# Two attentions in one kernel: the products with v move in front of the turns, and each group's last steps move a unit or two later

## The chip, the cores and the metric

The kernel is one program on one NeuronCore of a Trainium2 chip. TensorE, VectorE, ScalarE, GpSimd and the DMA queues run their own instruction lists, written out by hand, and meet only at semaphores. The metric is the device time of one execution in microseconds; smaller is better. The kernel before takes 2598.61 us (median of 3 runs, 2598.22 to 2599.84).

## The reference

The reference is a stack of three transformer-like layers over 512 latent tokens and 256 context tokens of width 1024. The change touches only its two softmax attentions:

```python
def one_block(qi):                       # 128 queries of one head
    s = einsum('bqhgd,bkhd->bhgqk', qi, k) * scale
    p = softmax(s, axis=-1)
    return einsum('bhgqk,bkhe->bqhge', p, v)
```

- The first layer (GQA) has 16 heads of 64. The 512 latent tokens attend to all 768 keys, the 256 context tokens to the 256 context keys.
- The second layer (MLA) has 16 heads. The 512 latent tokens attend to 768 keys.

Projections, MLPs, layer norms and the third layer (gated linear attention, mLSTM and an S5 state space) make up the rest of the time and are not changed.

## The kernel before, in words

A **unit** is one head and one block of 128 queries. MLA has 64 units, all with 768 keys. GQA has 96: 64 latent ones with 768 keys and 32 context ones with 256, in the order latent, latent, context. Four units of one kind that share a block of queries form a **group**. Operands are kept as two bf16 halves (high and low), so most products are three matmuls (lines 326, 327, 328).

Each unit passes through these steps:

| step in the code | engine | work for a unit with 768 keys | line |
|---|---|---|---|
| `scores` S | TensorE | 128x768 scores into a pair of PSUM banks | 1062, 1063 (GQA), 326 to 328 (MLA) |
| `largest` | VectorE | the negated row maximum | 1167 |
| `exponent` | ScalarE | exp of the scores, into one of three buffers | 1117, 1121 |
| `turn` T | TensorE | six 128x128 transposes, in two parts of three, one PSUM bank each | 1074 |
| `high` | ScalarE | the high half of each part, from PSUM | 1128 |
| `low` | VectorE | the low half of each part, which frees that part's bank | 1173 |
| `weigh` W | TensorE | 18 small products with v, into the group's bank | 326 to 328 |

After the fourth unit of a group come `divide` (VectorE, lines 1154 or 1156 and 1161), `out_turn` (TensorE, two transposes, line 1092), `out_high` (ScalarE, 1132) and `out_low` (VectorE, 1178), which frees the bank of `out_turn`.

The **bank rings** set what may run ahead. `bank(e, ring, name)` takes the next bank of a ring in turn and makes TensorE wait until its last user is freed. The ring "T" has two banks, 4 and 5, and serves the parts of `turn` and the `out_turn` of a group alike. The ring "S" has two pairs (0, 1) and (2, 3). "O" is bank 6 and "O2" bank 7. A latent unit's turn takes both T banks, a context unit's one, an `out_turn` one.

Each engine has its own loop over steps `i`, and the order inside a step is the order of its queue. With u for the last unit of a group, the kernel before has:

- TensorE (lines 1095 to 1103): S(i), T(i-2), W(i-3), then `out_turn` where i-6 = u.
- ScalarE (1134 to 1143): `exponent`(i-1), `high`(i-2), a quarter of a weight tile in four steps (i = 6, 10, 14, 18), `out_high` where i-6 = u.
- VectorE (1180 to 1190): `divide` where i-4 = u, `largest`(i), `low`(i-2), a quarter in the same four steps, `out_low` where i-6 = u.

Of the kernel before, what the change touches and what calls it, by code (L numbers as in the profile page):

```python
# [131 lines left out]
def build(nc, a, out):  # L132
    ctx = ExitStack()
    with ctx:
# [851 lines left out]
        class Pass:  # L986


            def __init__(self, tag, qtiles, keys, OT, q, k, v, O, sums, stacked):
                self.tag, self.qtiles, self.keys, self.OT = tag, qtiles, keys, OT  # L990
                self.q, self.k, self.v, self.O, self.sums0 = q, k, v, O, sums

                self.stacked, self.width = stacked, 65 if stacked else 64
                self.nq, self.nk = len(qtiles), keys[1] // 128
                self.parts = [(0, 3), (3, 6)] if self.nk == 6 else [(0, self.nk)]
# [20 lines left out]
        class Attention:  # L1016


            def __init__(self, tag, order, P, PT):
                self.tag, self.order, self.P, self.PT = tag, order, P, PT  # L1020
                self.n = len(order)
                self.steps = self.n + 7

            def scores_at(self, u):
                return at(("S", self.tag, u), self.order[u][0].keys[1])
# [24 lines left out]
        def attention_pe(e, Q):  # L1050
            t = Q.tag

            def scores(u):
                A, r = Q.order[u]
                h, j = A.unit(r)
                q, k = A.q(e, h, A.qtiles[j]), A.k(e, h)
                bank(e, "S", ("S", t, u))
                k0, n = A.keys
                for c0, c1 in [(0, 512), (512, n)] if n > 512 else [(0, n)]:
                    o, x = at(("S", t, u), c1 - c0, c0), [x[:, k0 + c0:k0 + c1] for x in k]  # L1060
                    if A.stacked:
                        e.matmul(o, q, x[0], start=True, stop=False)
                        m = e.matmul(o, q, x[1], start=False, stop=True)
                    else:
                        m = mm3(e, o, q, x, True, True)
                m.then_inc(pe.sem, pe.mark(("S", t, u)))

            def turn(u):
                A, _ = Q.order[u]
                ac.wait_ge(e, ("exp", t, u))  # L1070
                for i, (a_, b_) in enumerate(A.parts):
                    bank(e, "T", ("T", t, u, i))
                    for k in range(a_, b_):
                        m = e.transpose(at(("T", t, u, i), 128, (k - a_) * 128), Q.p(u)[:, k * 128:(k + 1) * 128], ident)  # L1074
                    m.then_inc(pe.sem, pe.mark(("T", t, u, i)))

            def weigh(u):
                A, r = Q.order[u]
                h, j = A.unit(r)
                if r % 4 == 0:  # L1080
                    bank(e, A.O, ("O", A.tag, r // 4))
                o = at(("O", A.tag, r // 4), A.width, A.width * (r % 4))
                dv.wait_ge(e, ("low", t, u))
                for k in range(A.nk):
                    m = mm3(e, o, [Q.PT[u % 3][:, i, k, :] for i in range(2)], A.v(e, k, h), k == 0, k == A.nk - 1)
                m.then_inc(pe.sem, pe.mark(("W", t, u), *([("O", A.tag, r // 4)] if r % 4 == 3 else [])))

            def out_turn(A, g):
                bank(e, "T", ("OT", A.tag, g))
                dv.wait_ge(e, ("out", A.tag, g))  # L1090
                for k in range(2):
                    m = e.transpose(at(("OT", A.tag, g), 128, k * 128), A.OT[g % 2][:, k * 128:(k + 1) * 128], ident)
                m.then_inc(pe.sem, pe.mark(("OT", A.tag, g)))

            for i in range(Q.steps):
                if i < Q.n:
                    scores(i)
                if 0 <= i - 2 < Q.n:
                    turn(i - 2)
                if 0 <= i - 3 < Q.n:  # L1100
                    weigh(i - 3)
                if whole := Q.group_at(i - 6):
                    out_turn(*whole)


# [2 lines left out]
        def attention_act(e, Q, done):  # L1108
            t = Q.tag

            def exponent(u):
                A, r = Q.order[u]
                if u > 2:
                    pe.wait_ge(e, ("T", t, u - 3, Q.last_part(u - 3)))
                dv.wait_ge(e, ("max", t, u))
                if A.stacked:
                    e.activation(Q.p(u), Q.scores_at(u), EXP, bias=Q.largest(u)).then_inc(ac.sem, ac.mark(("exp", t, u), ("free", ("S", t, u))))  # L1117
                    return
                if r > 7:
                    dv.wait_ge(e, ("out", A.tag, r // 4 - 2))  # L1120
                e.activation(Q.p(u), Q.scores_at(u), EXP, bias=Q.largest(u), accum_out=A.sums(r)).then_inc(ac.sem, ac.mark(("exp", t, u), ("free", ("S", t, u))))  # L1121

            def high(u):
                for i in range(len(Q.order[u][0].parts)):
                    if u > 2:
                        pe.wait_ge(e, ("W", t, u - 3))
                    pe.wait_ge(e, ("T", t, u, i))
                    e.activation(Q.pt(u, i)[0], Q.turned_at(u, i), COPY).then_inc(ac.sem, ac.mark(("high", t, u, i)))  # L1128

            def out_high(A, g):  # L1130
                pe.wait_ge(e, ("OT", A.tag, g))
                e.activation(A.out(g)[0], at(("OT", A.tag, g), 256).rearrange("p (k n) -> p k n", n=128), COPY).then_inc(ac.sem, ac.mark(("out high", A.tag, g)))

            for i in range(Q.steps):
                if 0 <= i - 1 < Q.n:
                    exponent(i - 1)
                if 0 <= i - 2 < Q.n:
                    high(i - 2)
                if i in QUARTERS:
                    pe.wait_ge(e, done)  # L1140
                    high_quarter(e, QUARTERS[i])
                if whole := Q.group_at(i - 6):
                    out_high(*whole)

        def attention_dve(e, Q):
            t = Q.tag

            def divide(u, A, g):

                sums = A.sums(4 * g, 4)  # L1150
                ac.wait_ge(e, ("exp", t, u))
                if A.stacked:
                    pe.wait_ge(e, ("O", A.tag, g))
                    e.reciprocal(sums, A.O_at(g)[:, :, 64]).then_inc(dv.sem, dv.mark())
                else:
                    e.reciprocal(sums, sums).then_inc(dv.sem, dv.mark())
                    pe.wait_ge(e, ("O", A.tag, g))
                if g > 1:
                    pe.wait_ge(e, ("OT", A.tag, g - 2))
                dv.wait_ge(e)  # L1160
                e.tensor_tensor(A.OT[g % 2].rearrange("p (h n) -> p h n", n=64), A.O_at(g)[:, :, 0:64], sums.unsqueeze(2).to_broadcast([128, 4, 64]), MUL).then_inc(dv.sem, dv.mark(("out", A.tag, g), ("free", ("O", A.tag, g))))

            def largest(u):
                if u > 3:
                    ac.wait_ge(e, ("exp", t, u - 4))
                pe.wait_ge(e, ("S", t, u))
                e.tensor_reduce(Q.largest(u), Q.scores_at(u), AX.X, MAX, negate=True).then_inc(dv.sem, dv.mark(("max", t, u)))  # L1167

            def low(u):
                for i in range(len(Q.order[u][0].parts)):  # L1170
                    hi, lo = Q.pt(u, i)
                    ac.wait_ge(e, ("high", t, u, i))
                    e.tensor_tensor(lo, Q.turned_at(u, i), hi, SUB).then_inc(dv.sem, dv.mark(("low", t, u), ("free", ("T", t, u, i))))  # L1173

            def out_low(A, g):
                hi, lo = A.out(g)
                ac.wait_ge(e, ("out high", A.tag, g))
                e.tensor_tensor(lo, at(("OT", A.tag, g), 256).rearrange("p (k n) -> p k n", n=128), hi, SUB).then_inc(dv.sem, dv.mark(("o", A.tag, g), ("free", ("OT", A.tag, g))))

            for i in range(Q.steps):  # L1180
                if whole := Q.group_at(i - 4):
                    divide(i - 4, *whole)
                if i < Q.n:
                    largest(i)
                if 0 <= i - 2 < Q.n:
                    low(i - 2)
                if i in QUARTERS:
                    low_quarter(e, QUARTERS[i])
                if whole := Q.group_at(i - 6):
                    out_low(*whole)  # L1190


# [930 lines left out]
        def mla_pe(e):  # L2123
            heads_pe(e)
            attention_pe(e, MLA)
# [1610 lines left out]
```

## Time and profile before

| | before |
|---|---|
| median of 3 runs | 2598.61 us |
| the profiled execution | 2602.68 us |
| its span | 2600.9 us |
| TensorE matmul busy | 2470.7 us (95%) |
| VectorE busy | 1630.2 us (63%) |
| ScalarE busy | 1039.5 us (40%) |
| mean granted TensorE clock | 0.985 of full speed |

The time of an execution is its span plus 1.8 us outside it. The two attentions fill the span from 179 to 362 us (GQA) and from 1109 to 1262 us (MLA). In the trace, PE is the matmul and PEld the weight load ahead of it. The time in brackets behind a row is the idle time just before it and what ended that.

### The profile page before, as it was taken

What the parts mean: (1) busy time and instruction counts of PE and PEld (TensorE: products, weight loads), DVE (VectorE), ACT (ScalarE), POOL (GpSimd) and SP (SyncE); (2) the same over time, 40 slices, a digit from 0 to 9 for tenths busy, and PEclk for the clock granted to TensorE, in tenths of its full rate; (3) what the DMA queues carried; (4) which work ended last, traced back from release to release, by engine and by line L of the source; (5) the groups of instructions that cost most, each with busy time, mean ns of one, the idle gap of its engine ahead of it and who ended that gap; (6) DMA issues with size and microseconds to landing.
All of it is one profiled execution on the core that took longest, in us unless ns stands there. A gap on an engine that the chain in (4) does not pass through costs nothing.

```text
span 2600.9 us, 39022 instructions
## 1 busy us (share of the span) xinstructions
PE 2470.7 (95%) x16410; PEld 1439.0 (55%) x16410; DVE 1630.2 (63%) x2478; ACT 1039.5 (40%) x1666; POOL 727.5 (28%) x789
## 2 busy tenths in 40 slices
PE   6999999999999999899989999999999999999999
PEld 3566665665565585477554444735644445744444
DVE  4469964868844345888677744479966774533341
ACT  3457753433311124677444322333352234523230
POOL 0210000649999603300041000016454552011100
PEclk8999999999999999999999999999999999999999
DMA  6520014124444331300236645232212323233340
GB/s 246 180 80 18 2 50 146 52 88 146 154 154 162 138 122 47 106 18 2 61 102 201 203 163 178 79 106 69 86 57 92 111 100 118 66 95 99 99 146 33
DMA packets 224046, 271.40 MB, mean 104 GB/s; under 512 B 10047, under 2 KB 181438, under 8 KB 220798
## 3 DMA queue, kind: packets, MB, share of 16 engines
q1 hardware_dynamic: 217486, 247.05, 29.5%
q0 software_dynamic: 5280, 18.64, 2.0%
q8 instruction: 129, 2.11, 0.3%
q10 hardware_dynamic: 1104, 3.21, 0.3%
q14 instruction: 47, 0.39, 0.0%
HBM read 252.62 MB, written 10.49 MB: 101 GB/s over the span
## 4 chain that ended last, share of the span: by engine, by line
PE 74%; DVE 15%; ACT 6%; issue 2%; DMA 2%; POOL 1%; ACTq 0%; DVEq 0%; POOLq 0%
PE PS L326 22%; PE PS L328 21%; PE PS L327 21%; PE PS L1074 2%; DVE WB L305 2%; DVE SM L1167 2%; ACT WB L293 2%; DVE AR L1173 2%; ACT AR L1117 1%; DMA WS<-in_w_ada 1%; DVE X L1450 1%; PE PS L558 1%; DVE GT L1459 1%; DMA WS<-in_mlp_w 1%; DMA EB<-in_s_lam_im 1%
## 5 line engine op out<-in xcount | busy, mean ns | idle before, releaser
L326 PE MATMUL PS<-H,WB 128*128 128x512 bf16 (+1 forms) x1976 | 686.4, 347 | 20.8 <-DVE WB L305 8.0
L327 PE MATMUL PS<-H,WB 128*128 128x512 bf16 (+1 forms) x1976 | 685.5, 347 | 0.0
L328 PE MATMUL PS<-H,WB 128*128 128x512 bf16 (+1 forms) x1976 | 684.9, 347 | 0.0
L305 DVE TENSOR_TENSOR WB<-WS,WB 128x2048 bf16<-128x2048 f32 (+2 forms) x154 | 348.2, 2262 | 265.6 <-ACT WB L293 265.5
L293 ACT ACTIVATE WB<-WS 128x2048 bf16<-128x2048 f32 (+2 forms) x154 | 275.1, 1787 | 399.5 <-PE PS L328 222.9
L326 PE MATMUL PS<-AR,WB 128*128 128x512 bf16 (+1 forms) x1140 | 369.9, 324 | 8.9 <-DVE WB L305 8.1
L327 PE MATMUL PS<-AR,WB 128*128 128x512 bf16 (+1 forms) x1140 | 369.6, 324 | 0.0
L328 PE MATMUL PS<-AR,WB 128*128 128x512 bf16 (+1 forms) x1140 | 369.6, 324 | 0.0
L326 PEld LDWEIGHTS PS<-H,WB 128*128 128x128 bf16 x1976 | 194.9, 99 | 214.3 <-issue 22.0
L328 PEld LDWEIGHTS PS<-H,WB 128*128 128x128 bf16 x1976 | 194.9, 99 | 167.1 <-issue 3.0
L327 PEld LDWEIGHTS PS<-H,WB 128*128 128x128 bf16 x1976 | 195.0, 99 | 163.3 <-issue 5.3
L1538 POOL TENSOR_TENSOR X<-X,STAT 128x256 f32<-128x256 f32 x56 | 57.5, 1062 | 660.7 <-DVE H L1467 660.7
L326 PEld LDWEIGHTS PS<-AR,WB 128*128 128x128 bf16 x1140 | 111.6, 98 | 97.0 <-issue 13.0
L658 DVE SCALAR_TENSOR_TENSOR ACC<-WS,SIL,ACC 128x512 f32<-128x512 f32 x196 | 152.6, 797 | 14.5 <-DMA WS<-in_w_ada 8.9
L327 PEld LDWEIGHTS PS<-AR,WB 128*128 128x128 bf16 x1140 | 111.7, 98 | 72.1 <-issue 2.5
L328 PEld LDWEIGHTS PS<-AR,WB 128*128 128x128 bf16 x1140 | 111.6, 98 | 71.8 <-issue 0.6
L1173 DVE TENSOR_TENSOR AR<-PS,AR 128x384 bf16<-128x384 f32 x288 | 143.3, 534 | 12.1 <-ACT AR L1128 10.0
L1167 DVE TENSOR_REDUCE SM<-PS 128x1 f32<-128x768 f32 x160 | 135.2, 846 | 10.7 <-PE PS L328 6.1
L1128 ACT ACTIVATE AR<-PS 128x384 bf16<-128x384 f32 x288 | 127.2, 477 | 34.3 <-PE PS L1074 29.9
L1438 DVE SCALAR_TENSOR_TENSOR X<-PS,MOD,X 128x256 f32<-128x256 f32 (+1 forms) x56 | 33.4, 596 | 170.7 <-PE PS L328 170.6
L1599 ACT ACTIVATE GT<-PS 128x512 f32<-128x512 f32 x96 | 50.2, 523 | 194.3 <-PE PS L328 185.1
L326 PE MATMUL PS<-AR 128*128 128x65 bf16 (+1 forms) x616 | 108.0, 233 | 1.9 <-ACT GT L1121 0.9
(497 smaller groups left out, 4293.1 us busy)
## 6 DMA issues: line engine op xcount, KB each, us to landing
WS<-in_mlp_w SPq DMA_DIRECT2D x64, 1024.0 KB, 5.7
WS<-in_w_ada SPq DMA_DIRECT2D x40, 1024.0 KB, 5.1
WS<-in_w_in SPq DMA_DIRECT2D x26, 1024.0 KB, 5.1
WS<-in_ada_w SPq DMA_DIRECT2D x24, 1024.0 KB, 5.2
WS<-in_ffn_w_in SPq DMA_DIRECT2D x44, 512.0 KB, 4.9
WS<-in_ffn_w_out SPq DMA_DIRECT2D x10, 1024.0 KB, 4.9
AR<-in_w_ada SPq DMA_DIRECT2D x8, 1024.0 KB, 13.0
e_scratch<-EB POOLq DMA_DIRECT2D x16, 512.0 KB, 3.1
```

The lines of the kernel that those rows point to most:

```text
L293: e.activation(hi, staged_as(i, hi), COPY).then_inc(ac.sem, ac.mark(("hi", i)))
L305: e.tensor_tensor(lo, staged_as(i, lo), hi, SUB).then_inc(dv.sem, dv.mark(("lo", i)))
L326: e.matmul(out_, l[0], r[0], start=start, stop=False)
L327: e.matmul(out_, l[0], r[1], start=False, stop=False)
L328: return e.matmul(out_, l[1], r[0], start=False, stop=stop)
L658: e.scalar_tensor_tensor(out=y, in0=w[:, x, :], scalar=s, in1=y, op0=MUL, op1=ADD).then_inc(dv.sem, dv.mark(("weighed", r, t // 2, v, k), ...
L1074: m = e.transpose(at(("T", t, u, i), 128, (k - a_) * 128), Q.p(u)[:, k * 128:(k + 1) * 128], ident)
L1128: e.activation(Q.pt(u, i)[0], Q.turned_at(u, i), COPY).then_inc(ac.sem, ac.mark(("high", t, u, i)))
L1167: e.tensor_reduce(Q.largest(u), Q.scores_at(u), AX.X, MAX, negate=True).then_inc(dv.sem, dv.mark(("max", t, u)))
L1173: e.tensor_tensor(lo, Q.turned_at(u, i), hi, SUB).then_inc(dv.sem, dv.mark(("low", t, u), ("free", ("T", t, u, i))))
L1538: e.tensor_tensor(seg(X, f, p), seg(X, f, p), factor_at(p), MUL).then_inc(po.sem, po.mark(("over", tag, f, p), ("factor read", tag)))
L1599: e.activation(x, ps(bank_of[("w1", i), m, s], SEG[s][1]), RELU).then_inc(ac.sem, ac.mark(("relu", i, n), ("free", (("w1", i), m, s))))
```

## The change

`Attention.steps` grows by two, and the order inside a step changes on the three engines:

```diff
-                self.steps = self.n + 7
+                self.steps = self.n + 9
@@ attention_pe
                 if i < Q.n:
                     scores(i)
+                if 0 <= i - 4 < Q.n:
+                    weigh(i - 4)
                 if 0 <= i - 2 < Q.n:
                     turn(i - 2)
-                if 0 <= i - 3 < Q.n:
-                    weigh(i - 3)
-                if whole := Q.group_at(i - 6):
+                if whole := Q.group_at(i - 7):
                     out_turn(*whole)
@@ attention_act
-                if 0 <= i - 1 < Q.n:
-                    exponent(i - 1)
-                if 0 <= i - 2 < Q.n:
-                    high(i - 2)
+                if 0 <= i - 3 < Q.n:
+                    high(i - 3)
                 if i in QUARTERS:
                     pe.wait_ge(e, done)
                     high_quarter(e, QUARTERS[i])
-                if whole := Q.group_at(i - 6):
+                if whole := Q.group_at(i - 8):
                     out_high(*whole)
+                if 0 <= i - 1 < Q.n:
+                    exponent(i - 1)
@@ attention_dve
-                if whole := Q.group_at(i - 4):
-                    divide(i - 4, *whole)
+                if whole := Q.group_at(i - 5):
+                    divide(i - 5, *whole)
+                if 0 <= i - 3 < Q.n:
+                    low(i - 3)
                 if i < Q.n:
                     largest(i)
-                if 0 <= i - 2 < Q.n:
-                    low(i - 2)
                 if i in QUARTERS:
                     low_quarter(e, QUARTERS[i])
-                if whole := Q.group_at(i - 6):
+                if whole := Q.group_at(i - 8):
                     out_low(*whole)
```

No instruction, DMA, buffer or bank is added or removed. The waits inside each step's function stay as they were.

## Rows read from the trace of the kernel before

**Rows 1.** Stretches: start to end, length, busy time of each engine, clock, DMA.
```profile
260.00:280.00 20.00, 18.56 (x240) 13.38 (x238) 18.21 (x38) 15.72 (x31) 0.00 (x0) 1.00 0.01 2
1076.70:1085.50 8.80, 6.47 (x33) 3.04 (x31) 7.75 (x14) 4.05 (x8) 8.49 (x7) 1.00 0.31 74
1085.60:1092.40 6.80, 5.26 (x13) 1.94 (x14) 4.74 (x6) 2.60 (x5) 6.80 (x12) 0.50 0.90 294
1200.00:1220.00 20.00, 19.33 (x269) 15.69 (x268) 17.98 (x33) 16.08 (x37) 0.00 (x0) 1.00 0.01 2
```

**Rows 2.** Waits of the GQA attention: total us, times, longest.
```profile
PEld PS L1074 <- DVE AR L1173: 26.4, 85, 1.0
```

**Rows 3.** Timeline of the MLA attention around an out_turn: start, length, engine, operation.
```profile
1202.90 0.38 PE L326 MATMUL PS<-AR 128*128 128x512 bf16 x1
...
1203.77 0.69 PEld L1074 LDWEIGHTS PS<-KM,GT 128*128 128x128 f32 x6
...
1204.40 0.87 ACT L1128 ACTIVATE AR<-PS 128x384 bf16<-128x384 f32 x2 [0.40 <-PE PS L1074]
...
1204.53 0.19 PE L326 MATMUL PS<-X,AR 128*128 128x64 bf16 x1
...
1204.95 1.01 DVE L1173 TENSOR_TENSOR AR<-PS,AR 128x384 bf16<-128x384 f32 x2
...
1205.03 0.19 PE L328 MATMUL PS<-EB,AR 128*128 128x64 bf16 x1
...
1205.56 0.20 PEld L1092 LDWEIGHTS PS<-KM,AR 128*128 128x128 f32 x2 [0.46 <-DVE AR L1173]
...
1205.83 0.38 PE L326 MATMUL PS<-AR 128*128 128x512 bf16 x1
...
1207.01 0.96 DVE L1167 TENSOR_REDUCE SM<-PS 128x1 f32<-128x768 f32 x1
...
1207.88 1.01 DVE L1173 TENSOR_TENSOR AR<-PS,AR 128x384 bf16<-128x384 f32 x2
```

**Rows 4.** Chain of waits in the GQA attention: the same turn, 12 units apart.
```profile
240.59 1.01 PE PS L1074 x6
...
263.33 1.01 PE PS L1074 x6
```

**Rows 5.** Timeline of the GQA attention: spacing and hand-over of each kind of operation.
```profile
267.01 0.42 DVE L1178 TENSOR_TENSOR H<-PS,H 128x256 bf16<-128x256 f32 x1
...
267.35 0.41 DVE L1167 TENSOR_REDUCE SM<-PS 128x1 f32<-128x256 f32 x1
267.49 0.31 PEld L1074 LDWEIGHTS PS<-KM,AR 128*128 128x128 f32 x3 [0.26 <-DVE H L1178]
267.66 0.91 ACT L1128 ACTIVATE AR<-PS 128x384 bf16<-128x384 f32 x2
...
268.18 1.02 DVE L1173 TENSOR_TENSOR AR<-PS,AR 128x384 bf16<-128x384 f32 x2 [0.41 <-ACT AR L1128]
...
268.79 0.31 PEld L1074 LDWEIGHTS PS<-KM,AR 128*128 128x128 f32 x3 [0.20 <-DVE AR L1173]
...
269.12 0.95 DVE L1167 TENSOR_REDUCE SM<-PS 128x1 f32<-128x768 f32 x1
...
269.38 0.95 ACT L1128 ACTIVATE AR<-PS 128x384 bf16<-128x384 f32 x2 [0.45 <-PE PS L1074]
...
271.05 0.96 DVE L1167 TENSOR_REDUCE SM<-PS 128x1 f32<-128x768 f32 x1
...
272.04 0.90 ACT L1117 ACTIVATE AR<-PS,SM 128x768 f32<-128x768 f32 x1 [0.39 <-DVE SM L1167]
...
272.26 0.17 DVE L1154 RECIPROCAL SM<-PS 128x4 f32<-128x4 f32 x1
...
272.81 0.41 DVE L1167 TENSOR_REDUCE SM<-PS 128x1 f32<-128x256 f32 x1
272.84 0.86 ACT L1128 ACTIVATE AR<-PS 128x384 bf16<-128x384 f32 x2
```

**Rows 6.** Lines in both attentions: count, busy us, mean ns, idle before.
```profile
L321 DVE TENSOR_TENSOR WB<-WS,WB 128x512 bf16<-128x512 f32 x8 | 5.5, 682 | 0.0
```

## The prediction, made before the change was run

> **What bounds the kernel now.** I read the table of stretches first, to see which engine limits each attention [rows 1]. Then came the waits and the timelines of one steady period of each. In the MLA attention TensorE is the bound. A unit takes S 0.97, T 0.65 and W 0.53 us, matmul start to matmul start: 1202.90 to 1204.53 is S and T together, 1204.53 to 1205.06 the 18 products [rows 3]. These follow each other without a gap, 2.155 us a unit. The only gap stands ahead of `out_turn`: its weight load waits 0.50 us (1205.06 to 1205.56) for a T bank, which VectorE's `low` must free. With 0.27 us for `out_turn` a group of four takes 4 x 2.155 + 0.27 + 0.50 = 9.39 us.
>
> In the GQA attention no engine is full. Twelve units (8 latent, 4 context, 3 groups) take 22.74 us [rows 4]. TensorE waits 26.4 us in all on `low` ahead of a turn [rows 2]. VectorE's own spacings are 0.94 us for a latent `low` (268.18 to 269.12), 0.87 for its maximum (the next one [rows 3] shows), about 0.34 for each context operation and for `out_low`, 0.55 for `divide` (272.26 to 272.81) [rows 5]. That gives 8 x 1.81 + 4 x 0.68 + 3 x 0.55 + 3 x 0.34 = 19.9 of 22.74 us. The rest is hand-overs between the engines.
>
> **What the edits really move.** A step's boundary is nothing to an engine; only the order of its queue counts. So I write out each queue across the steps.
>
> - ScalarE before: `exponent`(i-1), `high`(i-2), `exponent`(i), `high`(i-1). After: `high`(i-3), `exponent`(i-1), `high`(i-2), `exponent`(i). It is the same sequence, cut at another place. I cost this edit at nothing.
> - VectorE likewise: `largest` and `low` alternate with the same offset before and after. Nothing again.
> - TensorE before: T(i-2), W(i-3), S(i+1), T(i-1). After: T(i-2), S(i+1), W(i-3), T(i-1). S and W trade places; from one turn to the next there is still one S and one W. Scores are ready 0.53 us earlier, and W has 0.97 us more slack. W waits for nothing that its turn did not already wait for (both need `low`), and in MLA no S or W waits now, so the trade gives nothing there. In GQA it can take away VectorE's wait for scores. The timeline has it small, and the walk below counts it.
> - `divide` moves one instruction later, behind `largest`(u+4). The next group's first W still comes S and T (1.62 us) after W(u). `divide` starts 0.87 us later than before and ends in time. Nothing.
> - `out_turn` before stood behind T(u+4) and W(u+3). Now it stands directly behind T(u+5). This is the first cost.
> - `out_low` before stood right behind `low`(u+4). Now it stands behind `low`(u+5) and then `largest`(u+8), whose scores TensorE issues only after that `out_turn`. This is the second cost.
>
> **MLA, step by step.** Let 0 be the weight load of T(u+5). A turn's load to `high` is 0.63 us, `high` to `low` 0.55, `low` to the load that its bank frees 0.61, together 1.79 [rows 3]. `out_turn` takes the bank of the first part of the turn just issued, so it starts at 1.79 in both kernels. Before, TensorE had T and W to issue meanwhile and was ready at 1.29; now only T, and is ready at 0.76. The wait grows from 0.50 to 1.03: **0.53 us more a group**.
>
> The scores S(u+8) then start at 1.79 + 0.27 = 2.06. `largest`(u+8) starts 1.18 later (1205.83 to 1207.01) at 3.24, and VectorE is idle until then. `out_low` follows 0.87 later, at 4.11. The bank is free for a load 0.48 after its start (267.01 to 267.49 [rows 5]), at 4.59. The second part of T(u+6) needs that bank. Without a wait its load would go at 2.06 + 0.97 + 0.53 - 0.11 + 0.33 = 3.78, and by matmul starts (3.89 against 4.59, plus some 0.05 that a stalled load isn't overlapped) the loss is **0.75 us a group**. Before, this didn't arise, since `out_low` was done 0.9 us after `out_turn` began.
>
> What follows catches up with nothing, since TensorE is the bound: T(u+7), T(u+8) and T(u+9) come 2.155 us apart with their inputs ready. A period becomes 9.39 + 0.53 + 0.75 = 10.67 us. 14 groups have scores behind their `out_turn`; the last two fall into the drain. 14 x 1.28 = 17.9 us. Four steps convert a quarter of a weight tile (0.68 us on VectorE [rows 6]). These now stand ahead of `low`, beside the wait for scores. From their place I take 0.3 us less for each, -1.2 us, with 0 and -2.7 (all four hidden) as bounds. MLA: **+16.7 us**.
>
> **GQA, step by step.** Here stalls overlap with other waits, so I walked a period of 12 units by the spacings of [rows 3, 5]. The hand-overs: turn's load to `high` 0.59, `high` to `low` 0.52, `low` to load 0.61, `out_low` to load 0.48, maximum to `exponent` 0.99, `exponent` to the next `high` 0.80. For scores to maximum I take 0.86: MLA's 1.18 less a third of 0.97, as GQA scores are four matmuls and not six. `out_turn` costs 0.19 here. Before, the `out_turn` of the groups that end on the 5th and 11th unit of a period stood behind a context unit's turn, which takes one bank only, so that the other was long free; only the third waited. Now all three stand right behind a latent turn. The path that ends last, from `high` of one latent unit to the same 12 units on:
>
> - through the first `out_turn`, scores, maximum, `out_low`, second part of the next turn: 0.52 + 0.61 + 0.19 + 0.86 + 0.87 + 0.48 + 0.59 + 0.52 = 4.64;
> - VectorE and ScalarE in turn up to the next latent `low`: 0.47 + 0.99 + 0.80 + 0.52 = 2.78;
> - 0.94 + 0.87 + 0.55 (`divide`) + 0.94 + 0.99 + 0.80 + 0.52 = 5.61;
> - through the second `out_turn`, as the first: 4.12;
> - through the third, whose wait runs beside the second's: 0.47 + 0.87 + 3 x 0.34 + 0.55 = 2.91;
> - 0.94 + 0.87 + 0.94 + 0.99 + 0.80 = 4.54.
>
> The sum is 24.6 us against 22.74: **+1.86 us a period**. There are 8 periods, and the last is half drain: 7.5 x 1.86 = **+14.0 us**. Its bounds: 0 if the slack in this attention takes up both waits (26.4 us of waiting stand there), +20 if each of the 22 groups with scores behind costs 0.9, between the one wait and both of MLA.
>
> **Sum.** The profiled execution of 2602.68 us would become 2602.7 + 16.7 + 14.0 = 2633.4. It lies 4.1 us above the median of the runs, so the median becomes 2598.6 + 30.7 = **2629.3 us**. What follows each attention starts later by as much; the edits leave all DMAs alone, and the DMA share in both is 0.01 [rows 1], so no transfer is late.
>
> **A rule against the trace.** In MLA matmuls are busy 19.33 of 20 us and weight loads 15.69 [rows 1], and the unit's matmuls start without a gap [rows 3]. The Trainium skill (Perfetto Trace Analysis, Identifying the Most-Contended Engine) says that matmul busy time tells little of how near TensorE is to its limit, and that the busy share of weight loads, beside the FLOPs used, does. By that share, 78%, TensorE would have a fifth of its time to spare and an added wait of 1.28 us a group would be free, which is the second rival below. The spacing of the starts speaks against it.
>
> **Rivals.**
>
> - *One wait only* (+11 us, 2610). If `out_low` is not late, because scores come sooner than I count, MLA loses 14 x 0.53 = 7.4 and GQA about half of its slack-covered part, 4 us. For it: the second wait is a difference of two sums of six terms. Against: it is 0.7 us, far over their error. Chance 0.17.
> - *Waits hidden* (+0, 2598.6). The idle time of an engine with spare time takes them. Only GQA offers that. Chance 0.04.
> - *Faster* (2575 to 2590). The swap of S and W ends the GQA waits: at VectorE's 19.9 us a period, 8 x 2.84 = 23 us go, and it decides if VectorE's waits there came from late scores and not from the banks. It gives up to 2576 if MLA stays, 2592 if MLA loses 16.7. Against: TensorE's 26.4 us of waits are on `low`, that is on banks. Chance 0.07.
> - *The clock falls* (2650). In both attentions it is 1.00, at 18.56 busy us of 20 in GQA. It fell to 0.50 for 6.8 us behind a stretch with 2.3 idle us in 8.8 [rows 1]; my longest new gap is 1.0 us. If six of the 14 MLA groups ran such a stretch at half clock, each losing half of 6.8 us, 20 us come on top: 2650. The Trainium skill (TensorE: Matmul & The Clock Gate, A second HAM failure mode: psum-queue depth-cycling) says that short idles between groups of matmuls, from cycling PSUM banks, can make the clock swing between its levels; the trace shows such idles in GQA with no fall. Chance 0.06.
>
> **Chances.** The forecast has 0.66. The range for 8 in 10 reaches to the one-wait case and 11 us up: 2609 to 2640. A measurement here can't tell less than 0.2% (5.2 us) from no change. Faster 0.07, same 0.04, slower 0.89.
>
> **What would show it.** After: `out_turn`'s load waits about 1.0 us instead of 0.46 on `low` in MLA; a turn's second load waits 0.7 us on `out_low`, 14 times or more; the MLA period is 10.7 us and the GQA period 24.6; maxima of MLA wait for scores about 1.1 us once a group; clock 1.00 in both. Busy times stay. An `out_turn` that waits no longer than now, or a GQA period under 22.7, would prove me wrong.

## The result and the profile after

The changed kernel takes 2633.24 us (median of 4 runs, 2632.5 to 2634.67), the kernel before 2599.23 us beside it. The ratio is 1.0123 (95% interval 1.0111 to 1.0135): 1.2% slower. The forecast was 2629.3 us, 30.7 us on top of the median of the kernel before. The median grew by 34.0 us and the profiled execution by 30.8, from 2602.68 to 2633.45. That the second number meets the forecast to 0.1 us is partly luck: runs of the kernel before, taken for the experiments, lie between 2597.8 and 2605.8 us. The lengths of the two attentions, below, are the better test.

Where the time went, by stretch: I take the length of an attention from the start of its first maximum to the end of its last `out_low`.

| | GQA | MLA |
|---|---|---|
| before | 186.3 us | 156.3 us |
| after | 200.5 us | 173.4 us |
| difference, forecast | +14.2, +14.0 | +17.1, +16.7 |

Together +31.3 us; what lies outside both changed by -0.6 us between the two profiled executions. The same two stretches as in [rows 1], from the table of stretches of the changed kernel (start:end, length, busy us of PE, PEld, DVE, ACT, POOL, clock, DMA share, GB/s):

```profile
260.00:280.00 20.00, 16.06 (x208) 12.20 (x206) 15.83 (x33) 13.78 (x29) 0.00 (x0) 1.00 0.01 2
1200.00:1220.00 20.00, 17.32 (x223) 13.55 (x221) 15.75 (x28) 13.53 (x32) 0.00 (x0) 1.00 0.01 2
```

All engines are less busy in both, and the clock stays at 1.00, its upper level of 2.4 GHz. So the added time is idle time and not slower work.

**MLA after.** The timeline around one `out_turn` of the changed kernel, weight loads first, then VectorE. It answers to [rows 3].

```profile
1210.61 0.64 PEld L1074 LDWEIGHTS PS<-KM,STAT 128*128 128x128 f32 x6
1212.34 0.20 PEld L1092 LDWEIGHTS PS<-KM,AR 128*128 128x128 f32 x2 [1.08 <-DVE AR L1173]
1214.08 0.32 PEld L1074 LDWEIGHTS PS<-KM,GT 128*128 128x128 f32 x3
1215.13 0.31 PEld L1074 LDWEIGHTS PS<-KM,GT 128*128 128x128 f32 x3 [0.73 <-DVE H L1178]
1216.99 0.64 PEld L1074 LDWEIGHTS PS<-KM,GT 128*128 128x128 f32 x6
1219.18 0.64 PEld L1074 LDWEIGHTS PS<-KM,STAT 128*128 128x128 f32 x6
1221.37 0.64 PEld L1074 LDWEIGHTS PS<-KM,GT 128*128 128x128 f32 x6
```

```profile
1211.72 1.02 DVE L1173 TENSOR_TENSOR AR<-PS,AR 128x384 bf16<-128x384 f32 x2 [0.30 <-ACT AR L1128]
1213.79 0.96 DVE L1167 TENSOR_REDUCE SM<-PS 128x1 f32<-128x768 f32 x1 [1.04 <-PE PS L328]
1214.66 0.42 DVE L1178 TENSOR_TENSOR H<-PS,H 128x256 bf16<-128x256 f32 x1
...
1225.41 0.42 DVE L1178 TENSOR_TENSOR H<-PS,H 128x256 bf16<-128x256 f32 x1
```

Both new waits are there, one behind the other. The turn at 1210.61 is loaded in one piece. `out_turn` right behind it waits 1.08 us for `low` (0.46 before). Scores follow it, so VectorE has nothing to do for 1.04 us until 1213.79, does the maximum, and only then `out_low`. The next turn's second half, at 1215.13, waits 0.73 us for that `out_low`. From one `out_low` to the next is 10.75 us (1214.66 to 1225.41), where the prediction had 10.67. Over the whole attention the second wait stands there 14 times.

**GQA after.** The waits of the whole stretch (engine and line, what it waited for, us in total, times, longest), against 26.4 us of waits on `low` ahead of a turn in [rows 2]:

```profile
PEld PS L1092 <- DVE AR L1173: 19.8, 22, 1.3
PEld PS L1074 <- DVE H L1178: 16.2, 15, 1.7
...
PEld PS L1074 <- DVE AR L1173: 7.9, 34, 0.5
```

The waits of the turns on `low` fell by 18.5 us, those of `out_turn` on `low` and of the turns on `out_low` took their place. VectorE in this stretch, the same two operations 12 units apart:

```profile
265.48 0.96 DVE L1167 TENSOR_REDUCE SM<-PS 128x1 f32<-128x768 f32 x1 [0.72 <-PE PS L1063]
266.36 0.41 DVE L1178 TENSOR_TENSOR H<-PS,H 128x256 bf16<-128x256 f32 x1
...
290.18 0.96 DVE L1167 TENSOR_REDUCE SM<-PS 128x1 f32<-128x768 f32 x1 [0.72 <-PE PS L1063]
291.06 0.42 DVE L1178 TENSOR_TENSOR H<-PS,H 128x256 bf16<-128x256 f32 x1
```

The period is 24.70 us (265.48 to 290.18), forecast 24.6. Periods of 24.70 and 24.78 us alternate.

The six legs of the prediction's walk can be read off the same period. These rows are where they begin and end, from one `high` to the same one 12 units on:

```profile
263.23 0.86 ACT L1128 ACTIVATE AR<-PS 128x384 bf16<-128x384 f32 x2
267.93 0.56 DVE L1173 TENSOR_TENSOR AR<-PS,AR 128x384 bf16<-128x384 f32 x1 [0.70 <-ACT AR L1128]
270.88 1.02 DVE L1173 TENSOR_TENSOR AR<-PS,AR 128x384 bf16<-128x384 f32 x2
275.91 1.02 DVE L1173 TENSOR_TENSOR AR<-PS,AR 128x384 bf16<-128x384 f32 x2 [0.69 <-ACT AR L1128]
280.10 0.56 DVE L1173 TENSOR_TENSOR AR<-PS,AR 128x384 bf16<-128x384 f32 x1 [0.70 <-ACT AR L1128]
282.87 1.02 DVE L1173 TENSOR_TENSOR AR<-PS,AR 128x384 bf16<-128x384 f32 x2
287.93 0.86 ACT L1128 ACTIVATE AR<-PS 128x384 bf16<-128x384 f32 x2
```

They last 4.70, 2.95, 5.03, 4.19, 2.77 and 5.06 us; the prediction had 4.64, 2.78, 5.61, 4.12, 2.91 and 4.54. The path is the forecast one, but one `divide` (0.55 us) lies in the last leg and not in the third.

### The profile page after: what moved, and what is told of

Its sections match the earlier page's. It is cut to its first block, busy times and chain, and to the rows that moved or that the text cites. A ratio compares the mean times of both kernels' runs of the same rounds, so it can differ in the third digit from the quotient of the medians.

```text
span 2631.6 us, 39022 instructions
## 1 busy us (share of the span) xinstructions
PE 2471.7 (94%) x16410; PEld 1441.8 (55%) x16410; DVE 1631.4 (62%) x2478; ACT 1040.7 (40%) x1666; POOL 725.2 (28%) x789
## 4 chain that ended last, share of the span: by engine, by line
PE 71%; DVE 17%; ACT 6%; issue 2%; DMA 2%; POOL 1%; ACTq 0%; DVEq 0%; POOLq 0%
PE PS L326 21%; PE PS L328 21%; PE PS L327 21%; DVE SM L1167 3%; DVE AR L1173 2%; DVE WB L305 2%; PE PS L1074 2%; ACT WB L293 2%; ACT AR L1128 1%; ACT AR L1117 1%; DMA WS<-in_w_ada 1%; DMA WS<-in_mlp_w 1%; DVE X L1450 1%; PE PS L558 1%; DVE GT L1459 1%
```

## The experiments

Eight kernels were run. Each ratio is against runs of the kernel before on the same chip. The columns GQA and MLA are the lengths of the attentions in us in the profiled execution, taken as above; they separate effects that the total, with the runs of one kernel 2 to 10 us apart, can't. "Before" stands for the three sets of runs beside e1 to e4, e5 to e7 and e8; the changed kernel's ratio is against the 2599.23 us above. The MLA period is the steady one, without quarters.

| | median | ratio (95% interval) | GQA | MLA | MLA period |
|---|---|---|---|---|---|
| before | 2601.19 to 2601.72 in three sets | | 186.3 | 156.3 | 9.39 |
| after | 2633.24 | 1.0123 (1.0111 to 1.0135) | 200.5 | 173.4 | 10.75 |
| e1 | 2614.58 | 1.0050 (1.0035 to 1.0065) | 192.9 | 163.6 | 10.04 |
| e2 | 2603.54 | 1.0012 (1.0002 to 1.0021) | 180.9 | 165.2 | 10.04 |
| e3 | 2611.1 | 1.0038 (1.0023 to 1.0053) | 200.5 | 149.5 | 9.04 |
| e4 | 2591.52 | 0.9965 (0.9952 to 0.9977) | 186.3 | 148.7 | 8.87 |
| e5 | 2589.7 | 0.9956 (0.9944 to 0.9968) | 180.9 | 150.0 | 8.97 |
| e6 | 2582.46 | 0.9935 (0.9923 to 0.9947) | 174.8 | 150.0 | 8.97 |
| e7 | 2583.22 | 0.9933 (0.9921 to 0.9945) | 174.8 | 149.9 | 8.97 |
| e8 | 2582.6 | 0.9923 (0.9910 to 0.9937) | 174.9 | 148.7 | 8.87 |

### e1: the changed kernel, out_low in front of the maximum

```diff
                 if 0 <= i - 3 < Q.n:
                     low(i - 3)
+                if whole := Q.group_at(i - 8):
+                    out_low(*whole)
                 if i < Q.n:
                     largest(i)
...
-                if whole := Q.group_at(i - 8):
-                    out_low(*whole)
```

> The changed kernel with one edit: VectorE does out_low in front of largest in its step, and not behind it, so that it no longer waits for the scores behind out_turn. Theory (two waits, 0.5 and 0.75 us a group): the second wait goes, the first stays. MLA period 10.75 -> about 10.0 us (-10.5 us over 14 groups), a turn's second load no longer waits on out_low, the wait of out_turn's load stays at 1.1 us; GQA period 24.7 -> about 22.9 (-13 us). Total about 2610 us (2604 to 2618). Rival (one wait only: out_turn behind the turn is the whole cost, out_low's place costs nothing): unchanged, 2633.

Measured: 2614.58 us. In the timeline of its weight loads in MLA the first wait stays and the second is gone; the turn behind `out_turn` is loaded in one piece again:

```profile
1206.30 0.64 PEld L1074 LDWEIGHTS PS<-KM,GT 128*128 128x128 f32 x6
1208.02 0.20 PEld L1092 LDWEIGHTS PS<-KM,AR 128*128 128x128 f32 x2 [1.08 <-DVE AR L1173]
1209.77 0.64 PEld L1074 LDWEIGHTS PS<-KM,GT 128*128 128x128 f32 x6
```

The second wait is shown, and its price with it: 9.8 us in MLA (173.4 to 163.6, 0.71 us a period), 7.6 in GQA, where I had expected 13. The one-wait rival falls.

### e2: the kernel before, scores and products exchanged

```diff
                 if i < Q.n:
                     scores(i)
+                if 0 <= i - 4 < Q.n:
+                    weigh(i - 4)
                 if 0 <= i - 2 < Q.n:
                     turn(i - 2)
-                if 0 <= i - 3 < Q.n:
-                    weigh(i - 3)
```

> The kernel before with one edit: on TensorE the products with v (now of unit i-4) stand in front of the turn, so that scores and products trade places; every other step keeps its place. out_turn then stands directly behind T(u+4), out_low right behind low(u+4). Theory: only the first wait grows (MLA period 9.39 -> 9.9, +7.5 us); in GQA two of three out_turns stand behind a context unit's turn and wait for nothing, the swap may give back a little (0 to -5 us) and divide now waits some 0.2 us for its products. Total about 2604 us (2599 to 2610). Rival (the swap itself, products too late, is what costs): the whole +34 us, 2633. Second rival (the swap is a gain in GQA, VectorE's waits for scores go): below 2594.

Measured: 2603.54 us. MLA loses 8.9 us (period 10.04, as in e1), since `out_turn` is right behind a turn here too. GQA gains 5.4 us: TensorE's waits on `low` ahead of a turn are 6.1 us in the whole stretch, as the grouped line of its turns shows (the figures behind the bar are busy us and mean ns, then idle time and what ended it).

```profile
L1074 PEld LDWEIGHTS PS<-KM,AR 128*128 128x128 f32 x448 | 46.5, 140 | 12.9 <-DVE AR L1173 6.1 <-ACT AR L1128 1.2 <-DVE H L1178 0.7
```

So the exchange itself is a gain in GQA, hidden in the changed kernel by the two waits. My "0 to -5" was right in sign and just short in size. The 20 us less of waits are not the gain, since others grew: those of `out_turn` on `low` are 9.4 us, against 4.9 before.

VectorE's queue shows where the period became shorter. First the kernel before, then e2, the same four operations of a period:

```profile
264.52 1.01 DVE L1173 TENSOR_TENSOR AR<-PS,AR 128x384 bf16<-128x384 f32 x2
265.58 0.96 DVE L1167 TENSOR_REDUCE SM<-PS 128x1 f32<-128x768 f32 x1
266.46 0.41 DVE L1173 TENSOR_TENSOR AR<-PS,AR 128x256 bf16<-128x256 f32 x1
267.01 0.42 DVE L1178 TENSOR_TENSOR H<-PS,H 128x256 bf16<-128x256 f32 x1
```

```profile
264.49 1.01 DVE L1173 TENSOR_TENSOR AR<-PS,AR 128x384 bf16<-128x384 f32 x2
265.42 0.95 DVE L1167 TENSOR_REDUCE SM<-PS 128x1 f32<-128x768 f32 x1
266.28 0.42 DVE L1173 TENSOR_TENSOR AR<-PS,AR 128x256 bf16<-128x256 f32 x1
266.61 0.42 DVE L1178 TENSOR_TENSOR H<-PS,H 128x256 bf16<-128x256 f32 x1
```

The maximum follows `low` after 0.93 us instead of 1.06, which happens three times a period. `out_low` follows a context unit's `low` twice a period, after 0.33 us each time instead of 0.55 and 0.70. Its `out_turn` no longer stands behind the products, and ScalarE's waits for it before `out_high` fall from 12.2 to 6.9 us in the stretch. That is 0.37 and 0.60 us a period; other spacings grow by 0.2, and the period falls from 22.73 to 21.97 us. No run separates the two.

The one `out_turn` of a period that waits 1.08 us still stands behind a latent turn, the others behind a context unit's:

```profile
276.30 0.20 PEld L1092 LDWEIGHTS PS<-KM,AR 128*128 128x128 f32 x2 [0.27 <-DVE AR L1173]
277.50 0.64 PEld L1074 LDWEIGHTS PS<-KM,AR 128*128 128x128 f32 x6
279.22 0.20 PEld L1092 LDWEIGHTS PS<-KM,AR 128*128 128x128 f32 x2 [1.08 <-DVE AR L1173]
```

### e3 and e4: out_turn of MLA in a bank of its own

The same edit in the changed kernel (e3) and in the kernel before (e4). The ring "side" is bank 7, which MLA doesn't use.

```diff
             def out_turn(A, g):
-                bank(e, "T", ("OT", A.tag, g))
+                bank(e, "side" if A.tag == "mla" else "T", ("OT", A.tag, g))
```

> The changed kernel with one edit: in MLA out_turn takes bank 7, which no one uses there, instead of a bank of ring T. GQA as changed. Theory: both waits of MLA are waits for that bank, so both go: MLA period 10.75 -> 8.9 us (4 x 2.155 + 0.27), -26 us over 14 groups, total about 2607 us (2602 to 2612). The late place of out_low then costs nothing. Rival (VectorE's 1.04 us without work once a group, or ScalarE's order, is what costs): MLA stays above 10 us a period, total above 2620.

> The kernel before with the same edit, out_turn of MLA in bank 7. Theory: its 0.50 us wait goes, MLA period 9.39 -> 8.9 us, -7.5 us: 2591 us (2588 to 2594). With both theories of the bank right, MLA takes the same time here as in the changed kernel with the same edit, whatever the order of the steps. Rival (the 0.50 us is hidden elsewhere, VectorE becomes the bound): 2597 or more.

Measured: e3 2611.1 us, e4 2591.52 us. In MLA, e4 takes 7.6 us less than the kernel before, where I had expected 7.5. e3 takes 23.9 us less than the changed kernel, with `out_low` just as late in its queue as there. Its weight loads show none of the two waits:

```profile
1215.89 0.64 PEld L1074 LDWEIGHTS PS<-KM,GT 128*128 128x128 f32 x6
1218.08 0.64 PEld L1074 LDWEIGHTS PS<-KM,GT 128*128 128x128 f32 x6
1218.69 0.25 PEld L1092 LDWEIGHTS PS<-KM,AR 128*128 128x128 f32 x2
1220.48 0.64 PEld L1074 LDWEIGHTS PS<-KM,STAT 128*128 128x128 f32 x6
```

GQA is unchanged at 200.5 us, as its code is. So both costs of MLA are waits for one PSUM bank, shown by taking the bank away from the contest. With it, the two orders of steps are 0.17 us a period apart (9.04 and 8.87), which neither wait explains. e5 and e8 find 0.10 of it in the exchange. The other 0.07 stand at one turn of each group in e3: the turn after it starts 2.26 us later and not 2.19 (1213.63 to 1215.89). Why is not shown.

### e5: the exchange and the own bank

The edits of e2 and e4 together.

> The kernel before with scores and products exchanged on TensorE (products of unit i-4 in front of the turn) and out_turn of MLA in bank 7; nothing else moved. Theory (the exchange is free in MLA and a gain in GQA; the bank wait is the rest): MLA period 8.87 us as with the own bank alone, GQA period 21.97 us as with the exchange alone; total 2599 - 7.5 - 5.4 = about 2586 us (2583 to 2590), 0.5% below before. Rival (the exchange costs MLA something of its own, as the 9.04 us a period of the changed kernel with bank 7 may say): MLA period 9.04 or more, total 2589 or more.

Measured: 2589.7 us (2585.45 to 2592.89). GQA is 180.9 us, as in e2. MLA has a period of 8.97, between theory and rival: the exchange costs MLA 0.10 us a group. The total is at the upper edge of what the theory had (2583 to 2590), and the rival's "2589 or more" holds it too, so the period decides and not the total.

### e6: the context groups' out steps two later

```diff
+        def whole_at(Q, i):
+            for late in (6, 8):
+                whole = Q.group_at(i - late)
+                if whole and (whole[0].tag == "ctx") == (late == 8):
+                    return whole
...
-                if whole := Q.group_at(i - 6):
+                if whole := whole_at(Q, i):
                     out_turn(*whole)
```

and so for `out_high` and `out_low`, with `Attention.steps` at n + 9, on top of e5.

> As the last, and in GQA the context groups' out_turn, out_high and out_low come two steps later (i-8), so that all three out_turns of a period stand behind a context unit's turn, which takes one bank. Theory (a latent turn right ahead is what makes out_turn wait): the 1.08 us wait once a period goes, GQA period 21.97 -> about 21.2 us, total about 2580 us (2577 to 2585). Rival (GQA is bound by the hand-overs between VectorE and ScalarE, the wait is covered): period stays 21.9 to 22.0, total as the last.

Measured: 2582.46 us. All three `out_turn`s of a period are now behind a context unit's turn (line numbers are six higher here: 1080 is the turn, 1098 `out_turn`):

```profile
272.36 0.20 PEld L1098 LDWEIGHTS PS<-KM,AR 128*128 128x128 f32 x2 [0.26 <-DVE AR L1179]
...
277.29 0.20 PEld L1080 LDWEIGHTS PS<-KM,AR 128*128 128x128 f32 x2
277.53 0.20 PEld L1098 LDWEIGHTS PS<-KM,AR 128*128 128x128 f32 x2
...
282.47 0.20 PEld L1080 LDWEIGHTS PS<-KM,AR 128*128 128x128 f32 x2
282.70 0.20 PEld L1098 LDWEIGHTS PS<-KM,AR 128*128 128x128 f32 x2
```

The 1.08 us wait is gone, and 0.26 us at one of the three is left. `out_low` comes every 21.08 us for the same group of a period (273.43 to 294.51), forecast 21.2, against 21.95 in e5. GQA: 174.8 us. What stands ahead of `out_turn` in the bank ring sets its wait. This run shows it by itself; the changed kernel, which moves other steps too, agrees.

### e7: divide behind the maximum

```diff
-                if whole := Q.group_at(i - 4):
-                    divide(i - 4, *whole)
                 if i < Q.n:
                     largest(i)
+                if whole := Q.group_at(i - 4):
+                    divide(i - 4, *whole)
```

on top of e6.

> As the last, and divide stands behind largest in its step, where the changed kernel has it. Theory: with products later by one scores, divide waits for them by 0.1 to 0.25 us a group in front of largest; behind it it does not; 0 to 2 us less than the last, 2579 (2576 to 2584). Rival: the next group's first products wait for divide, 2 us or more slower than the last.

Measured: 2583.22 us against 2582.46 for e6 in the same set: no difference that can be measured. Its MLA period is 8.97 as in e6. So that part of the change costs nothing, as the prediction had it, and brings nothing.

### e8: the exchange in GQA alone

```diff
-                if 0 <= i - 4 < Q.n:
+                if t == "gqa" and 0 <= i - 4 < Q.n:
                     weigh(i - 4)
                 if 0 <= i - 2 < Q.n:
                     turn(i - 2)
+                if t == "mla" and 0 <= i - 3 < Q.n:
+                    weigh(i - 3)
```

on top of e6.

> The kernel with the context groups' out steps two later and out_turn of MLA in bank 7, but scores and products exchanged in GQA alone; MLA has the order of before. Theory: MLA period 8.87 us instead of 8.97 (with the exchange each unit takes 2.19 us from turn to turn instead of 2.155), 16 groups, -1.6 us, about 2581 us (2577 to 2585). Rival (the 0.10 us a group comes from elsewhere, or is given back in GQA): MLA period 8.97, no change in total.

Measured: 2582.6 us. The MLA period is 8.87, and MLA takes 1.3 us less than in e6; the total can't tell. TensorE's matmuls show where. First the order of e5 and e6, from e5's trace, then that of e8. Each pair is the six transposes of a turn and what follows them.

```profile
1203.18 0.85 PE L1074 MATMUL PS<-KM,GT 128*128 128x128 f32 x6
1203.87 0.38 PE L326 MATMUL PS<-AR 128*128 128x512 bf16 x1
```

```profile
1187.57 0.82 PE L1080 MATMUL PS<-KM,STAT 128*128 128x128 f32 x6
1188.23 0.19 PE L326 MATMUL PS<-X,AR 128*128 128x64 bf16 x1
```

Scores start 0.69 us after the turn ahead of them starts, products 0.66 us after it. Three units of a group are longer by 0.035 us, which makes the 0.10 us; the fourth, with `out_turn` in it, takes 2.41 us in both orders.

This kernel is, with e6 and e7, the fastest version: 0.77% under the kernel before (ratio 0.9923, interval 0.9910 to 0.9937).

## Why the prediction was right, step by step

- **MLA bound by TensorE, a stall counts in full.** Right. The attention grew by 17.1 us. 14 periods times (10.75 - 9.39) are 19.0, and the quarters gave back part: a period that holds one is 10.96 us (an `out_low` at 1149.73, the next at 1160.69) against 9.97 before (1129.59 to 1139.55 there). So a quarter costs 0.21 us instead of 0.57, 0.36 less, where I had taken 0.3. With four of them that makes 17.6; the last 0.5 us are not located.
- **The first wait, 0.53 us a group.** The idle time ahead of `out_turn` went from 0.46 to 1.08, +0.62. e1, which keeps this wait alone, has a period 0.65 us above before. 0.10 of that is the exchange, below, which leaves 0.55. The own bank says the same: it takes 0.52 off the period of before and 1.07 off that of e2.
- **The second wait, 0.75 us.** 0.71 by e1 against the changed kernel. It came about as written: the maximum waits 1.04 us for scores that stand behind `out_turn`.
- **The same sequences on ScalarE and VectorE, at nothing.** Not run alone. e2 has the old cut and e1 the new one, and their MLA periods are both 10.04 us, with the same waits. That agrees with it.
- **The exchange of scores and products, at nothing in MLA.** Wrong by a small size: with it a unit takes 2.19 us (1216.99 to 1219.18 to 1221.37 above), not 2.155, and 0.10 us a group in e5 against e8. It was some 1.3 us of 31 in all. The three terms, 0.55, 0.71 and 0.10, are the whole 1.36 us that the period grew by; the prediction had 0.53, 0.75 and nothing.
- **GQA, +14.0.** 14.2 measured. The walk's path is the one in the trace, and its legs are right but for the place of one `divide`. The period grew by 2.0 us and not 1.86, over seven whole periods and not 7.5, and these two small errors cancel. By the runs the parts are -5.4 for the exchange (e2), +12.0 for `out_turn` behind latent turns (e1 against e2, which also moves `divide` and the quarters; e7 has `divide` at nothing, the quarters were not run apart) and +7.6 for the late `out_low` (e1 against after). The prediction named the exchange as something that the walk counts and gave it no number; that it is worth 5.4 us by itself it didn't say.
- **Rivals.** One wait only: fell with e1. Waits hidden: in MLA TensorE had no time to spare, although its weight loads were busy for only 78% of the stretch. The Trainium skill's rule for that share (Perfetto Trace Analysis, Identifying the Most-Contended Engine), taken without the FLOPs used that it stands beside, would have misled here; the trace disagrees with it in this stretch of small products, and the start-to-start spacing decided. Clock: 1.00 in both. Faster: the gain that it names exists, and is e2's 5.4 us, but not in this change. The forecast gave it 0.07 because the waits were "on banks". They were on banks, and still most of them went with the exchange: a bank is freed by `low`, and `low` stands in VectorE's queue behind what waited there. Of the gain, earlier scores are the smaller part, 0.37 us a period. The larger, 0.60, comes from an `out_low` that waited for an `out_turn` behind the products, which this rival didn't name.

## What to carry to other kernels

Write the queues out across the steps before costing a change of offsets: most of a "unit later" can be the same sequence cut elsewhere, and the few operations that really trade places carry the whole effect. When a rare operation shares a ring of banks with the steady ones, look at what stands right ahead of it in that ring: here the same two transposes waited 0 to 0.3 us right behind a one-bank turn and 1.1 us right behind a two-bank one. Its evacuation belongs ahead of whatever must wait for work that is issued behind it.

## What the runs showed of the hardware

The six transposes of a turn cost TensorE a little more ahead of scores than ahead of small products: a unit repeats every 2.155 us in the order scores, turn, products (e8) and every 2.19 us in the order scores, products, turn (e5), with no wait listed in either. The 0.035 us lie behind the turn: the next matmul starts 0.69 us after the turn's first, instead of 0.66. The traces don't say why.
